# Decay rows of the state-space part: from a TensorE broadcast to a DMA from a DRAM scratch, masked on GpSimd

## The reference

```
a    = dt * (-exp(a_log))                       # 256 tokens x 32 heads
acum = cumsum(a, axis=tokens)
lmat = exp(where(causal, acum[t] - acum[s], -inf))   # per head, 256 x 256
cb   = C[g] @ B[g].T                            # per group, 256 x 256
y    = (cb * lmat * dt[s]) @ xs                 # per head, 64 wide
y    = (y + d_skip * xs) * silu(z)              # the gating product
y    = y * rsqrt(mean(y*y over the group) + eps) * norm_g
out  = y @ w_ssd_o                              # 2048 -> 1024
mixed = sigmoid(g_attn) * y_attn + sigmoid(g_ssd) * out
```

## Time and profile before

| | |
|---|---|
| median of three runs | 2816.48 us (2816.06 to 2816.95) |
| span of the profiled execution | 2814.9 us |
| TensorE busy | 2800.3 us (99%) |
| granted TensorE clock | 1.000 over the span |
| the stage around the change | 1332.20 us (W0 begins) to 1397.09 us (the product with `w_ssd_o` begins) |

### The profile page before, as it was taken

How to read it: one execution, slowest core, us unless ns; L and a number is a source line. 1 busy time by engine, 2 the same in 40 slices (tenths; PEclk the granted TensorE clock), 3 DMA queues, 4 the chain that set the end, 5 groups by cost and what they waited for, 6 DMA issues and landing times.

```text
span 2814.9 us, 42397 instructions
## 1 busy us (share of the span) xinstructions
PE 2800.3 (99%) x16834; PEld 2485.0 (88%) x16834; DVE 1952.1 (69%) x3377; ACT 1624.4 (58%) x2784; POOL 345.9 (12%) x314
## 2 busy tenths in 40 slices
PE   9999999999999999999999999999999999999999
PEld 7888888888988888899889999999888889988997
DVE  6657765776676676768866998677555566766775
ACT  6544655755665564566745445776555555655663
POOL 0000000000010002000002445894000000000000
PEclk9999999999999999999999999999999999999999
DMA  7554556466436555445164554434555574536454
GB/s 229 191 178 159 181 194 227 135 202 221 148 124 194 202 189 181 135 156 187 61 224 166 183 182 160 136 131 161 193 192 193 194 246 137 180 110 209 147 195 149
DMA packets 270485, 491.25 MB, mean 175 GB/s; under 512 B 10880, under 2 KB 181248, under 8 KB 261584
## 3 DMA queue, kind: packets, MB, share of 16 engines
q1 hardware_dynamic: 268864, 480.08, 51.3%
q0 software_dynamic: 1424, 8.45, 0.8%
HBM read 486.41 MB, written 2.10 MB: 174 GB/s over the span
## 4 chain that ended last, share of the span: by engine, by line
PE 94%; DVE 4%; ACT 1%; issue 0%; DMA 0%; POOL 0%; DVEq 0%; POOLq 0%; ACTq 0%
PE ps L659 41%; PE ps L747 11%; PE ps L589 8%; PE ps L585 8%; PE ps L586 8%; PE ps L746 6%; PE ps L606 3%; PE ps L1268 2%; DVE halves L1543 1%; PE ps L1303 1%; PE ps L544 1%; DVE AR L2499 1%; PE ps L952 0%; PE ps L1322 0%; DVE AR L2495 0%
## 5 line engine op out<-in xcount | busy, mean ns | idle before, releaser
L2896 ACT ACTIVATE halves<-raw 128x1024 fp32r<-128x1024 f32 x828 | 870.1, 1058 | 695.5 <-PE ps L659 413.7
L1543 DVE TENSOR_TENSOR halves<-raw,halves 128x1024 fp32r<-128x1024 f32 x790 | 952.9, 1227 | 190.6 <-ACT halves L2896 187.4
L659 PE MATMUL ps<-halves,XX 128*128 128x512 f32 x2628 | 611.6, 391 | 0.4
L659 PEld LDWEIGHTS ps<-halves,XX 128*128 128x128 f32 x2628 | 489.9, 188 | 102.5 <-DVE XX L1581 1.0
L585 PE MATMUL ps<-XX,halves 128*128 128x256 f32 (+1 forms) x1960 | 486.1, 286 | 0.0
L586 PE MATMUL ps<-XX,halves 128*128 128x256 f32 (+1 forms) x1960 | 480.3, 283 | 0.0
L659 PE MATMUL ps<-halves,R 128*128 128x512 f32 x1908 | 439.9, 390 | 0.1
L659 PEld LDWEIGHTS ps<-halves,R 128*128 128x128 f32 x1908 | 356.7, 188 | 73.9 <-issue 0.6
L586 PEld LDWEIGHTS ps<-XX,halves 128*128 128x128 f32 (+1 forms) x1960 | 375.4, 192 | 0.1
L585 PEld LDWEIGHTS ps<-XX,halves 128*128 128x128 f32 (+1 forms) x1960 | 375.0, 191 | 0.1
L747 PE MATMUL ps<-XX,halves 128*128 128x512 f32 x1344 | 338.4, 393 | 0.6 <-DVE XX L1581 0.6
(11 more groups left out here) (390 smaller groups left out, 3180.8 us busy)
## 6 DMA issues: line engine op xcount, KB each, us to landing
raw<-in_w_ffn_in SPq DMA_DIRECT2D x88, 1024.0 KB, 5.1
raw<-in_w_in SPq DMA_DIRECT2D x74, 1024.0 KB, 5.3
raw<-in_uT SPq DMA_DIRECT2D x64, 1024.0 KB, 4.9
raw<-in_peer_v SPq DMA_DIRECT2D x64, 1024.0 KB, 4.9
raw<-in_w_ffn_out SPq DMA_DIRECT2D x44, 1024.0 KB, 4.9
raw<-in_w_up SPq DMA_DIRECT2D x24, 1024.0 KB, 5.8
raw<-in_mlstm_w_in SPq DMA_DIRECT2D x12, 1024.0 KB, 5.2
raw<-in_w_down SPq DMA_DIRECT2D x12, 1024.0 KB, 4.9
```

The costliest lines, as they stand in the source:

```text
L659: ins = mm(ps[:, bs[j * (width // 512) + h], :], xv[:, k0 + t, j * 128:(j + 1) * 128], wv[:, t, h * 512:(h + 1) * 512], start=first and q ...
L1543: te.tensor_tensor(lo, src, hi.bitcast(F32), ALU.subtract).then_inc(k.lo_made, 1)
L2896: act(hi, src, ACT.Copy).then_inc(k.hi_made, 1)
```

## The change: what it does

The cumulated rows (32 heads by 256) are written once from SBUF to a DRAM scratch `rows`. For each group, two transfers issued by GpSimd read the group's 4 rows back, each spread over all 128 partitions (`spread`: 4 x 256 and 4 x 128 columns, 512 KB and 256 KB). GpSimd masks the two diagonal blocks of 4 heads (`masked`, two `affine_select` of 128 x 512). ACT takes the exponential in place in SBUF. There is room for 4 groups, so the spread of group g+4 waits until the `sums` of group g are done on TensorE, and GpSimd waits for the transfer before it masks.

GpSimd also takes the product with z (`scaled_by_z`) and the low halves of W1, W3, W5 and W7. TensorE's `decay` and DVE's preparation of `acx` are gone. The step generator is replaced by plain loops that place whole groups ahead of the gate pieces: on TensorE groups 0 and 1 now stand ahead of W0.

```diff
-        self.on_pool = [0] + [self.u_first + n for n in range(1, SELECTED, 2)] + [self.next_four("m3") - 1]
+        self.misc_first = self.last_piece[self.chunk_at["misc"] - 1]
+        self.on_pool = [0] + [self.misc_first + n for n in range(1, 8, 2)] + [self.u_first + n for n in range(1, SELECTED, 2)] + [self.next_four("m3") - 1]
...
+    def decays(self, g):
+
+        return self.ar(8192 + g % 4 * 1536, 4, 384)
```

On TensorE:

```diff
-        def decay(h):
-            b = aux.take(pe, ("m2", "L", h))
-            pe.wait_ge(*s["vec"].need("m2.acx"))
-            mm(ps[:, b, 0:384], bc(k.sel[0:96, h:h + 1], [96, 128]), acx, start=True, stop=False)
-            ins = mm(k.diagonal(b), identb[:], mkq, start=False, stop=True)
-            filled(("m2", "L", h), ins)
...
-        for i in range(8):
+        done = 0
+        for i, until in enumerate((2, 2, 3, 4, 6, 8, 10, 10)):
             s0, k0 = i // 4 * 512, i % 4 * 2
-            if i == 2:
-                pe.begin(ssm(), 0)
-            if i in (2, 4, 6):
-                pe.advance(22)
+            for n in range(done, until):
+                if n < 8:
+                    group(n)
+                if n >= 2:
+                    sums(n - 2)
+            done = until
```

On GpSimd:

```diff
+    gp.wait_ge(*s["vec"].need("m2.rows"))
+    load(k.rows, k.AR[0:32, 24832:25088]).then_inc(*dma["rows_out"].mark("m2"))
+    def spread(g):
+        rows, L = k.rows[4 * g:4 * g + 4, :], k.decays(g)
+        if g == 0:
+            gp.wait_ge(*dma["rows_out"].need("m2"))
+        if g >= 4:
+            gp.wait_ge(*k.full["m2", "ssm", g - 4])
+        load(L[:, :, 0:256], rows.partition_broadcast(128)).then_inc(*dma[f"decay_in{g % 4}"].mark())
+        load(L[:, :, 256:384], rows[:, 128:256].partition_broadcast(128)).then_inc(*dma[f"decay_in{g % 4}"].mark(g))
+    def masked(g):
+        gp.wait_ge(*dma[f"decay_in{g % 4}"].need(g))
+        for o in (0, 256):
+            L = k.decays(g)[:, :, o:o + 128]
+            ins = nc.gpsimd.affine_select(L, L, [[0, 4], [1, 128]], ALU.is_ge, NEG, base=0, channel_multiplier=-1)
+        ins.then_inc(*s["pool"].mark(("m2.L", g)))
+    def scaled_by_z(g):
+        gs = slice(g * 256, g * 256 + 256)
+        gp.wait_ge(*s["gated"].need("m2.z"))
+        gp.wait_ge(*k.aux.gone(("m2", "ssm", g)))
+        nc.gpsimd.tensor_tensor(xs[:, :, gs], xs[:, :, gs], zz[:, :, gs], ALU.mult).then_inc(*s["pool"].mark(("m2.y", g)))
...
+    for g in range(4):
+        spread(g)
+    for g in range(4):
+        masked(g)
+    lower(k.misc_first + 1)
+    lower(k.misc_first + 3)
+    for g in range(8):
+        if g < 4:
+            spread(g + 4)
+        scaled_by_z(g)
+        if g >= 1:
+            root(g - 1)
+        if g < 4:
+            masked(g + 4)
+        if g in (0, 2):
+            lower(k.misc_first + 5 + g)
+    root(7)
```

On DVE:

```diff
-            in_three(acx[:, 0:256], ac)
-            te.tensor_copy(acx[:, 256:384], acx[:, 128:256].bitcast(F32)).then_inc(*step.mark("m2.acx"))
...
-            te.tensor_tensor(xs[:, :, gs], xs[:, :, gs], zz[:, :, gs], ALU.mult).then_inc(*s["part"].mark(("m2.y", g)))
...
+        def ssm(n):
+            if 2 <= n < 10:
+                sums(n - 2)
+            if n < 8:
+                group(n)
+                for h in range(4 * n, 4 * n + 4):
+                    decay(h)
+            if 3 <= n < 11:
+                moment(n - 3)
+            if n >= 4:
+                scale(n - 4)
+
+        done = 0
+        for until in (1, 2, 3, 4, 6, 8, 10, 10):
+            for n in range(done, until):
+                ssm(n)
+            done = until
             weights()
```

On ACT, in the decay of one head:

```diff
-            act(L[:, 0:256], ps[:, b, 0:256], ACT.Exp, bias=cc[:, 64 + h:65 + h])
+            a.wait_ge(*s["pool"].need(("m2.L", h // 4)))
+            act(L[:, 0:256], L[:, 0:256], ACT.Exp, bias=cc[:, 64 + h:65 + h])
```

More of the change, by code:

```diff
@@ L317, in __init__ @@
         (self.raw, self.halves, self.AR, self.part_at, self.XX, self.XF, self.cols, self.ident,
-         self.identb, self.sel, self.iota, self.mask, self.st, self.xsel, self.first, self.ps, self.spill) = mem
+         self.identb, self.sel, self.iota, self.mask, self.st, self.xsel, self.first, self.ps, self.spill, self.rows) = mem
         self.X = (self.XX[:, 0], self.XX[:, 1])
@@ L2331, in decay @@
         def decay(h):
-            L = L_[:, h % 8, :]
-            v.wait_ge(*aux.gone(("m2", "L", h)))
+            L = k.decays(h // 4)[:, h % 4, :]
+            v.wait_ge(*s["act"].need(("m2.L", h)))
             v.wait_ge(*k.right.gone(("m2", "cb", h // 4)))
@@ L2363, in scale, with moment @@
                     .then_inc(*s["chan"].mark(("m2", g, j)))
-        def ssm():
-            for g in range(11):
-                if g < 8:
-                    group(g)
-                    yield
-                    for r in range(4):
-                        decay(4 * g + r)
-                        yield
-                if 1 <= g < 9:
-                    sums(g - 1)
-                    yield
-                if 2 <= g < 10:
-                    n = 2 * (g - 2)
-                    v.wait_ge(*s["square"].need(("m2.y", g - 2)))
-                    te.tensor_scalar(cc[:, 128 + n:130 + n], cc[:, 128 + n:130 + n], 1.0 / 256, 1e-6,
-                                     ALU.mult, ALU.add).then_inc(*s["var"].mark(("m2.g", g - 2)))
-                    yield
-                if g >= 3:
-                    scale(g - 3)
-                    yield
-        for i in range(8):
-            if i == 2:
-                v.begin(ssm(), 0)
-            if i in (2, 4, 6):
-                v.advance(22)
+        def moment(g):
+            n = 2 * g
+            v.wait_ge(*s["square"].need(("m2.y", g)))
+            te.tensor_scalar(cc[:, 128 + n:130 + n], cc[:, 128 + n:130 + n], 1.0 / 256, 1e-6,
+                             ALU.mult, ALU.add).then_inc(*s["var"].mark(("m2.g", g)))
+        def ssm(n):
[14 more added lines that the diff above has]
+            done = until
             weights()
-        v.finish()
+        ssm(10)
+        ssm(11)
         turned("m2.n", k.pair(8192, 16, lo=19456), lambda c: col("sn", c), n=16, banks=k.late)
@@ L3457, in sums, with ssm @@
             ins.then_inc(*s["square"].mark(("m2.y", g)))
-        def ssm():
-            for g in range(11):
-                if g < 8:
-                    yield
-                    for r in range(4):
-                        decay(4 * g + r)
-                        yield
-                if 1 <= g < 9:
-                    yield
-                if 2 <= g < 10:
-                    sums(g - 2)
-                    yield
-                if g >= 3:
-                    yield
+        def ssm(n):
+            if n < 8:
+                for h in range(4 * n, 4 * n + 4):
+                    decay(h)
+            if 3 <= n < 11:
+                sums(n - 3)
         gB, mx = k.ar(15360, 2, 1024), k.pair(4096, 8)
         a.wait_ge(*s["act"].need(("m2.conv", 30)))
-        for i in range(8):
-            if i == 2:
-                a.begin(ssm(), 0)
-            if i in (2, 4, 6):
-                a.advance(22)
+        done = 0
+        for i, until in enumerate((1, 2, 3, 4, 6, 8, 10, 10)):
+            for n in range(done, until):
+                ssm(n)
+            done = until
             weights()
@@ L3854, in memory @@
             ctx.enter_context(nc.psum_tensor("ps", [128, 8, 512], F32)),
[L3855 removed]
+            nc.dram_tensor("spill", (128, 2, 1024), F32, kind="Internal").ap(),
+            nc.dram_tensor("rows", (32, 256), F32, kind="Internal").ap())
 def tiles(a, p=128):
```

61 lines of the change are left out of this document (17 added, 44 removed).

## The result

The changed kernel takes 2828.92 us (median of five runs, 2824.58 to 2830.38) against 2816.30 (2816.06 to 2816.95) for the kernel before: 12.6 us slower, a ratio of 1.0043 with a 95% interval of 1.0030 to 1.0055. The span of the profiled execution is 2828.6 us, at a mean granted clock of 0.996 where it was 1.000.

What follows compares the result with a forecast made beforehand. TensorE was taken to bound the stage, DVE and ACT just keeping up. GpSimd's serial loop ends at 1390.6; plus 14.0, the product with w_ssd_o begins at 1404.6, 7.5 us later: 2816.5 + 7.5 = 2824.0 us, range 2811 to 2842.

Steps and rivals of the forecast that it cites:

- M: End of GpSimd's last mask: 1346.7 + 4 L + 8 m + 2 x 2.4 + c, forecast 1390.6.
- The stand in front of the first C B product: TensorE, no longer covered by W0 and W1, idles from 1332.20 to 1336.57 for the last convolved piece: 4.4 us.
- Groups 0 to 3 at nothing: Their spreads, issued some 60 us ahead of use, are hidden by the convolved projection and cost nothing.
- L: In GpSimd's loop, time from the first issue to the landing of both transfers of a spread: taken as 6.3 us.
- rival D: Spreads in short rows stay at 65 GB/s, each taking 13.8 us: 37.5 us more, 2854; chance 0.08.
- m: Time of one mask on GpSimd, eight in the loop: taken as 1.49 us, half the way from 0.57 to 2.41.
- c: GpSimd's port waits where ten loop operations may meet DVE: 0.2 us each, 2.0 us.
- The start of the loop: Spread of group 4 waits for group 0's sums: 1336.57 + C B products 1.9 + W0, W1 5.5 + 2.7 = 1346.7.
- in the loop DVE mostly waits for the same masks: Argument against a high price for the port between GpSimd and DVE during the loop of groups 4 to 7.
- The signs: Expected: 4.4 us TensorE stand, GpSimd waiting for spreads, TensorE waiting ahead of groups 5 to 7's sums, released by DVE.
- None of it is on the path: DVE's lost work (product with z, four low halves of 1.2 us, acx) is off the path once TensorE needn't wait.
- Rival C: Port between GpSimd and DVE: each of ten loop operations loses 0.8 us rather than 0.2, giving 2830; chance 0.16.

Runs made afterwards that it cites:

- b3: Kernel before with one more wait: W0 on TensorE waits for the last convolved piece; 2822.70 us, +5.6.
- e2: Changed kernel with the spreads of groups 1 to 3 each waiting for a later convolved piece; 2829.80 us, +12.8 on the kernel before.
- b1: Kernel before with only the product with z and the low halves of W1, W3, W5, W7 moved to GpSimd; 2820.11 us, +3.0.
- e5: Changed kernel with the four low halves and the product with z back on DVE; 2822.69 us, +5.6 on the kernel before.
- e4: Changed kernel with the low halves of W1, W3, W5, W7 back on DVE; 2823.40 us, +6.4 on the kernel before.
- e7: Changed kernel with DVE's decay products reading the C B product in PSUM, without the copy to SBUF; 2822.98 us, +6.3 on the kernel before.
- e1: Changed kernel with W0 and W1 ahead of the first C B products again on TensorE; 2826.73 us, +9.8 on the kernel before.
- c2: Changed kernel, low halves on DVE, W0 and W1 first, spreads paced, decay products from PSUM, square and groups reordered, z product on GpSimd; 2818.09 us.
- c3: c2 with the same work in another order on TensorE, ACT and DVE; 2814.21 us, -2.6 on the kernel before.

## Why the prediction was right in its number and wrong in a step

The forecast was 2824.0 and slower, the range 2811 to 2842; the time is 2828.9. That the number came near is luck in part. With M where it was measured (1386.1), the same sum would have put the product with w_ssd_o at 1400.1, 3.0 us later than before, and the time at 2819.5. Point by point:

- **The stand in front of the first C B product.** Predicted 4.4 us, measured 4.33, released by ACT. Its price was short of the clock: the stand costs 5.6 us in b3, 1.2 more than the 4.4 in the sum.
- **Groups 0 to 3 at nothing.** In the sum this held (e2: no difference). But the cover is thinner than I said: their transfers doubled the landing of the weight chunks.
- **L.** Taken 6.3, measured 5.1 to 5.6 in three groups and 7.7 in one, 23.8 us for the four instead of 25.2. The 13.8 us of rival D do not quite follow from its rows: 12.1 for the bytes, 1.5 left of the 3.5 us of the small spread and 0.5 for the second issue give 14.1.
- **m.** Taken 1.49, measured 0.63 undisturbed and 0.83 in the mean of the eight later masks. I had gone half the way to a two-input instruction; the row of 0.60 was the near one. With c, this is most of what the loop was shorter by: 6.7 us for the masks, disturbed ones included, instead of 11.9 + 2.0.
- **The start of the loop.** Taken 1346.7, measured 1351.1, when GpSimd issues the spread of group 4. About 1 us is the traces' different start. The projection ended 1.2 us later, counted from the fixed place, and the C B products, W0 and W1 behind the stand took 8.5 us (1338.86 to 1347.35) where the sum had 6.8; that is the slow clock.
- **M and what follows.** M was taken as 1390.6 and measured as 1386.1: the loop took 35.0 us instead of 43.9, and began 4.4 later. Then the product was to begin at M + 14.0; it began at M + 24.3. This is the step that failed: "in the loop DVE mostly waits for the same masks". DVE waited for its exponentials 0.5 us in the whole stage and was busy for 50.55 of 52 us. The loop did not set the end. Two errors partly cancel, M too late by 4.5 and what follows too short by 10.3. They leave 5.8 us in the profiled execution, which at 2830.36 was one of the slower of the five; by the median the forecast fell short by 4.9.
- **The signs.** TensorE did wait ahead of late sums, released by DVE's decay products (1.93 and 2.31 us), as the prediction had asked for. This sign could not tell the two causes apart: a DVE that waits for masks and a DVE that is slow look alike from TensorE. DVE's own waits tell them apart.
- **"None of it is on the path."** What I took off DVE was held to be worth nothing and to cost nothing. It cost more than it gave: 10.4 us went to GpSimd and DVE's other SBUF work grew by 12.1 (b1) to 16.6 us (36.6 + 6.9 against 22.0 + 4.9).
- **Rival C** named the mechanism, but on the wrong engine: it let GpSimd lose 0.8 us per operation. Its 2830 lies near the result by accident, since the loop that it lengthens was not the bound. DVE loses 1 to 2 us per operation of GpSimd (e5 against e4: 8.0 us for 8 products with z; e4 against the changed kernel: 6.0 for the 3 low halves in the stage). The row of 3.33 instead of 1.2 us had shown just that. The Trainium skill (SBUF — State Buffer, Who interferes with whom) says that a DVE instruction with two SBUF inputs contends with a GpSimd one that reads SBUF, and one with at most one SBUF input, outside the modes with two ports, does not; the changed kernel and e7 agree with the two halves (36.6 and 22.0 us). Among the operations that can enter such a mode it names the scales' (tensor_scalar), and b1 has them at 731 instead of 348 ns.
- **The decays off TensorE** (9.9 us less) gave nothing that can be seen: TensorE waited for DVE instead (2.29, 1.93 and 2.31 us in its timeline), with the slow clock behind. That is argued from the waits; no run has them alone.

How the 12.6 us divide: with the operations back on DVE (e5) 5.6 are left, and the stand alone costs 5.6 (b3). So by e5 7.0 us are the operations on GpSimd with the slow clock behind the waits that they cause. That the rest equals the stand is no proof that it is the stand, for e5 has other waits too, and each of the two figures is uncertain by some 2.5 us. In the kernel before, the same operations cost 3.0 us (b1), and with the stand's 5.6 that makes 8.6 of 12.6. The other 4.0 appear only when both come together. b1 had fewer meetings of the two engines and its clock never fell; that this is the reason is argued, not shown. The parts also overlap the other way: taking the stand out by itself gains only 2.8 (e1), and taking the hold-up of the decay products and the copies out by themselves gains 6.3 (e7), with new waits for banks in it.

What stays open: how much of the 7.0 us is the clock and how much the waits themselves. That the transfers and masks cost and gain nothing by themselves is worked out from e5 and b3; no run has them alone.

## What to carry to other kernels

Before work moves from one engine to another, read the busy share of both in the stage itself: an engine that is busy 54 of 61 us has little to give and is soon a bound, whatever its share of the whole span. A two-input operation on GpSimd is not free beside DVE instructions with both operands in SBUF; here it was beside those that keep one in PSUM. Reading a product where TensorE left it can be worth more than the offload, and saves the copy, but it holds the bank longer. A wait that is put on TensorE can cost more than its length (4.24 us of wait and 2.4 of slow clock in b3), so a transfer's or a neighbour's latency is better covered with gate pieces than stood through.

## What the runs showed of the hardware that I had not expected

- Stands of TensorE much shorter than the first one (4.33 us) were followed by a granted clock of one half: 2.29 us (a clock of 0.50 from 1374 to 1386 in the changed kernel), 1.61 us (c2, where one gate piece behind it took 4.50 us instead of 3.0) and 1.19 us (e4, 0.50 from 1375 to 1381). But the length of a stand does not decide alone: behind one of 1.60 us in e7 (1362.87) and one of 1.50 us in c3 (1391.52) the clock stayed at 1.00.
- An `affine_select` of 128 x 512 takes 0.63 us on GpSimd (up to 1.86 beside DVE's instructions with both operands in SBUF), a product of 128 x 512 1.3 us (0.69 on DVE), and the issue of a spread of four rows 0.78 us where another's took 0.53.
- Selects cost DVE little in all (its decay products took 22.6 us with them and 22.0 without), mostly because few products met one: the 3 that did took 0.62 to 0.80 us. The eight products with z beside them cost 8.0.
- Four spreads at once, 3 MB, took the weight chunks from 5.3 to 11.2 us; one at a time (e2) did not: the chunks landed in 5.3 us again, the spreads themselves in 6.6 and 7.2.
